# Second gate-and-up group of the second layer: each block by seven half-width block products instead of eight

## The chip, the cores and the metric

The kernel runs on one core of one Trainium2 chip. The metric is the time of one execution in microseconds; lower is better.

## The reference, cut to what matters

Two decoder layers over 512 tokens with 1024 features. Each has a mixer (attention) and then this feed-forward part, with 2816 hidden features:

```python
def swiglu(h, w_gate, w_up, w_down):
    return (jax.nn.silu(h @ w_gate) * (h @ w_up)) @ w_down

for l in range(DEPTH):
    ...
    h = x * (1.0 + sc2) + sh2
    y = swiglu(h, w_gate[l], w_up[l], w_down[l])
    x = layer_norm(ALPHA * x + (1.0 + gt2) * y, ln2_g[l], ln2_b[l])
```

## The kernel before, in words

**Data and splitting.** The input of the feed-forward part, transposed, lies in SBUF as `hT_hi` and `hT_lo` (128 partitions, 8 feature chunks `KD`, 512 tokens). Every operand of a matmul is split into a rounded high half and the remainder as low half, and a product is three matmuls: high by high, high by low, low by high (`split_product`, lines 663 to 665; `first_product`, line 1124, and `fresh_piece`, lines 727 to 732, do the same in another order). A weight piece is 128 by 1024 numbers, 512 KB. It comes by a DMA of the sync engine (SP, line 463) into one of the four slots of `w_raw`; ScalarE writes the high half `w_hi` (`convert`, line 1314; `feed`, line 1475), Vector the low half `w_lo` as raw minus high (`convert`, line 1590; `low_half` in `feed`, line 2012), and SP loads the piece four further on as soon as a piece's low half is there (`lo_ready`). TensorE marks a piece as used (`piece_used`), and only then is its slot of `w_hi` and `w_lo` written again.

**Order of the second layer's feed-forward part.** The hidden features are 22 blocks of 128, in a first group of 12 and a second of 10. Each group: `gate_up` (per block a gate piece and an up piece, each 8 chunks by 3 matmuls of 512 tokens), then two down phases, `down(l, g, 0)` and `down(l, g, 1)`, over 6 (second group 5) pieces each; a down piece is 24 matmuls of 512 columns. In a loop over pairs of blocks, `gate_up` leaves gate and up in four PSUM banks. ScalarE takes the Silu of the gate out of PSUM (line 1468) and converts the next pieces; Vector multiplies with the up block (line 2038), ScalarE rounds the result (line 1478), and Vector makes its low half (line 2043). After the first group Vector also adds the first norm's rows (`affine`, lines 1921 and 1922, with `g_row` and `b_row`), and after each down phase adds the four tiles to the residual (`residual`, lines 1845 and 1848).

**Queues.** Each engine's program is an order written out by hand; semaphores tie them. In the second layer GpSimd (POOL) has, after attention, the DMAs of the next norm's rows into `g_row` and `b_row` (`ln_rows`, lines 553 and 554) and small roots (line 496). Elsewhere it does elementwise work: the rotation of queries (`rope`, lines 426, 427, 432), the norm's rows (`affine`, lines 541 and 546) and sums of weights for the modulation (line 590). `ada_w`, a ring of four slots for modulation weights, isn't used any more in the second layer's feed-forward part.

## Time and profile before

| what | value |
|---|---|
| three runs | 1267.54, 1268.41, 1266.77 us; median 1267.54 |
| profiled execution | span 1267.1 us from the first to the last instruction; its own time beside that isn't given |
| second group of the second layer, matmuls | from about 1096.0 to 1204.8 us |
| down phases ahead of it | from about 1030 to 1096.0 us |
| instructions | 18297, of them 6362 matmuls with as many weight loads |

In rows of groups, "x20 | 24.5, 1226" is 20 instructions, 24.5 us busy, mean 1226 ns of one, and behind the next bar the idle time ahead of them and what ended it. In a timeline a row is a start and a length in us, the engine, the line of the kernel, the operation, what it writes and reads, and how many instructions are merged in it. PE is TensorE's matmuls, PEld its weight loads, DVE Vector, ACT ScalarE, POOL GpSimd, SPq the sync engine's DMA queue.

### The profile page before, as it was taken

The page shows a single profiled execution, that of the slowest core. Times are in us where ns is not written, and L with a number is a line of the kernel's source. Part 1 is how long each engine was busy: PE and PEld are TensorE (multiplying, and loading weights), DVE is VectorE, ACT ScalarE, POOL GpSimd, SP SyncE. Part 2 cuts the span into 40 slices and gives each one's busy share as a digit, 9 for nine tenths or more (in the row PEclk, how much of TensorE's full clock was granted, in tenths as well). Part 3 has the DMA queues.
Part 4 walks back from the last instruction along what each step waited for, and adds up shares of the span by engine and source line. Part 5 has one row for each costly group of instructions (what it writes and reads, how often), then busy time and mean ns, then how long its engine had stood idle before and what let it go on. Part 6 is the DMA issues. An engine that isn't in the chain of part 4 may idle for free. (4 is left out here: it accounts for less than half of the span.)

```text
span 1267.1 us, 18297 instructions
## 1 busy us (share of the span) xinstructions
PE 1230.2 (97%) x6362; PEld 1028.0 (81%) x6362; DVE 805.6 (64%) x1404; ACT 514.9 (41%) x1031; POOL 282.9 (22%) x285
## 2 busy tenths in 40 slices
PE   5999999999999999999999999899999999999997
PEld 4888887889888888888888688778988888888886
DVE  6899987777878774333776699756733355433338
ACT  4556668354333212222154566862533322222220
POOL 4247237501112010000007466670000000000000
PEclk9999999999999999999999999999999999999999
DMA  9872001424888553222523120111232223222211
GB/s 357 310 254 95 18 18 51 152 110 158 276 283 277 186 190 129 97 99 99 178 88 107 61 67 1 51 67 67 90 109 99 99 100 133 100 100 96 89 64 66
DMA packets 44849, 158.28 MB, mean 125 GB/s; under 512 B 5872, under 2 KB 5872, under 8 KB 44784
## 3 DMA queue, kind: packets, MB, share of 16 engines
q1 hardware_dynamic: 30528, 109.07, 24.6%
q0 software_dynamic: 12960, 47.19, 11.0%
q10 hardware_dynamic: 1296, 1.17, 0.3%
q8 instruction: 39, 0.64, 0.2%
q14 instruction: 26, 0.21, 0.0%
HBM read 155.31 MB, written 2.10 MB: 124 GB/s over the span
## 5 line engine op out<-in xcount | busy, mean ns | idle before, releaser
L663 PE MATMUL bank<-hT_hi,w_hi 128*128 128x512 f32 x640 | 249.4, 390 | 0.0
L665 PE MATMUL bank<-hT_hi,w_lo 128*128 128x512 f32 x640 | 249.0, 389 | 0.0
L664 PE MATMUL bank<-hT_lo,w_hi 128*128 128x512 f32 x640 | 249.0, 389 | 0.0
L2012 DVE TENSOR_TENSOR w_lo<-w_raw,w_hi 128x1024 fp32r<-128x1024 f32 x88 | 107.8, 1225 | 144.8 <-ACT w_hi L1475 144.8
L1314 ACT ACTIVATE w_hi<-w_raw 128x1024 fp32r<-128x1024 f32 x96 | 100.8, 1061 | 199.1 <-PE bank L665 184.7
L1475 ACT ACTIVATE w_hi<-w_raw 128x1024 fp32r<-128x1024 f32 x88 | 93.0, 1057 | 161.1 <-PE bank L665 155.8
L663 PE MATMUL bank<-w_hi,hT_hi 128*128 128x512 f32 (+2 forms) x392 | 148.0, 377 | 3.0 <-ACT pq L1352 2.0
L1590 DVE TENSOR_TENSOR w_lo<-w_raw,w_hi 128x1024 fp32r<-128x1024 f32 x88 | 114.1, 1311 | 56.0 <-ACT w_hi L1314 54.6
L665 PE MATMUL bank<-w_hi,hT_lo 128*128 128x512 f32 (+2 forms) x392 | 142.5, 364 | 0.0
L664 PE MATMUL bank<-w_lo,hT_hi 128*128 128x512 f32 (+2 forms) x392 | 142.4, 363 | 0.0
L664 PEld LDWEIGHTS bank<-hT_lo,w_hi 128*128 128x128 f32 x640 | 120.2, 188 | 24.9
L665 PEld LDWEIGHTS bank<-hT_hi,w_lo 128*128 128x128 f32 x640 | 120.1, 188 | 24.8
L663 PEld LDWEIGHTS bank<-hT_hi,w_hi 128*128 128x128 f32 x640 | 120.1, 188 | 24.8
L496 POOL TENSOR_TENSOR rs_out<-rs_in,minus_half 128x1 f32<-128x1 f32 x31 | 21.4, 690 | 366.6 <-DVE rs_in L1860 325.4
L663 PE MATMUL bank<-w_hi,gu_hi 128*128 128x512 f32 x264 | 102.9, 390 | 0.0
L665 PE MATMUL bank<-w_hi,gu_lo 128*128 128x512 f32 x264 | 102.7, 389 | 0.0
L664 PE MATMUL bank<-w_lo,gu_hi 128*128 128x512 f32 x264 | 102.7, 389 | 0.0
L2038 DVE TENSOR_TENSOR gu<-bank,silu_g 128x512 f32<-128x512 f32 x44 | 30.4, 692 | 95.8 <-PE bank L665 95.3
L663 PEld LDWEIGHTS bank<-w_hi,hT_hi 128*128 128x128 f32 x392 | 73.9, 188 | 21.5 <-issue 7.0
L1468 ACT ACTIVATE silu_g<-bank 128x512 f32<-128x512 f32 x44 | 26.3, 598 | 152.4 <-PE bank L665 145.9
L665 PEld LDWEIGHTS bank<-w_hi,hT_lo 128*128 128x128 f32 x392 | 73.8, 188 | 11.5
L664 PEld LDWEIGHTS bank<-w_lo,hT_hi 128*128 128x128 f32 x392 | 74.0, 189 | 9.9 <-issue 0.5
(220 smaller groups left out, 2209.9 us busy)
## 6 DMA issues: line engine op xcount, KB each, us to landing
w_raw<-in_weights SPq DMA_DIRECT2D x184, 512.0 KB, 3.5
ada_w<-in_w_ada POOLq DMA_DIRECT2D x76, 512.0 KB, 5.4
ada_w<-in_w_ada SPq DMA_DIRECT2D x4, 512.0 KB, 6.7
qT<-in_w_ada SPq DMA_DIRECT2D x4, 512.0 KB, 10.1
xs<-in_x SPq DMA_DIRECT2D x4, 512.0 KB, 16.6
g_row<-in_ln_row POOLq DMA_DIRECT2D x4, 512.0 KB, 5.2
b_row<-in_ln_row POOLq DMA_DIRECT2D x4, 512.0 KB, 6.3
trunk_out<-xs SPq DMA_DIRECT2D x8, 256.0 KB, 2.0
```

The source lines that it names most:

```text
L496: nc.gpsimd.tensor_tensor(rs_out[:, n:n + 1], rs_in[:, n:n + 1], minus_half[:], ALU.pow)\
L663: pe.matmul(dst, a_hi, b_hi, start=first, stop=False)
L664: pe.matmul(dst, a_hi, b_lo, start=False, stop=False)
L665: return pe.matmul(dst, a_lo, b_hi, start=False, stop=last)
L1314: nc.scalar.activation(w_hi[:, p % RING, :], w_raw[:, p % RING, :], ACT.Copy).then_inc(hi_ready, 1)
L1468: nc.scalar.activation(silu_g[:, f, :], bank[GU_BANK[g] + 2 * f][:], ACT.Silu)\
L1475: nc.scalar.activation(w_hi[:, s, :], w_raw[:, s, :], ACT.Copy).then_inc(hi_ready, 1)
L1590: nc.vector.tensor_tensor(w_lo[:, p % RING, :], w_raw[:, p % RING, :], w_hi[:, p % RING, :].bitcast(F32), ALU.subtract).then_inc(lo_ready, 1)
L2012: nc.vector.tensor_tensor(w_lo[:, s, :], w_raw[:, s, :], w_hi[:, s, :].bitcast(F32), ALU.subtract).then_inc(lo_ready, 1)
L2038: nc.vector.tensor_tensor(gu[:, f, :], bank[GU_BANK[g] + 2 * f + 1][:], silu_g[:, f, :], ALU.mult).then_inc(gu_ready, 1)
```

## The change

For the second layer's second group (10 blocks) `gate_up_seven` takes the place of `gate_up`. For each block the gate and up weights are seen as a 2 by 2 arrangement (gate or up, first or second half of the 1024 input features), the input as another (half of the features, half of the tokens). Eight block products of 4 chunks by 256 tokens become seven (the variant of Strassen's scheme with four sums on each side): p1 to p7 on G1, G2, U2 (halves of the weights as they are) and S1 to S4 (sums and differences of them), against halves of the input or its sums T1 to T4.

- GpSimd makes the input sums once (`input_sums`, ten operations of 1024 elements a partition, in `g_row`, `b_row` and other free space, before `ln_rows`), and four weight sums of 512 elements for each block (`weight_sums`). `ln_rows` comes behind them all.
- ScalarE and Vector split the input sums into halves (`split_input`, four each, set among the conversions of the down pieces), and for each block seven units of 512 elements (`unit`) in place of two pieces of 1024.
- TensorE does 7 products of 4 chunks by 3 matmuls of 256 columns for each block, written out without a loop; p1, p6, p7 and p4 accumulate in one bank. ScalarE copies the sum out of it after p1, p6 and p7 (`take_p1`, `take_p16`, `take_p167`), Vector adds those copies to the other products (`sum_gate1`, `sum_gate2`, `sum_up2`); Silu and multiply work on halves of 256 tokens.
- TensorE releases slots by waiting for a product of its own (`slots_used`), three times at the end.

The first layer and the first group run as before.

```diff
+SEVEN = (1,)
+SEVEN_F = FG[1]
+UNIT_ROWS = HALF
+COLS = SEQ // 2
+A_BANK, C_BANK, E_BANK = (0, 1), 2, 3
+def unit_order():
+    first = [("G1", 0), ("S2", 0), ("S3", 0), ("G2", 0), ("S1", 0), ("U2", 0)]
+    for f in range(SEVEN_F):
+        ahead = f + 1 < SEVEN_F
+        first += [("G1", f + 1)] if ahead else []
+        first += [("U2", f)] if f > 0 else []
+        first += [("S2", f + 1)] if ahead else []
+        first += [("S4", f)]
+        first += [("S3", f + 1), ("G2", f + 1), ("S1", f + 1)] if ahead else []
+    return first
+OWN_UNITS = [u for u in unit_order() if u[0] not in ("G2", "U2")]
+UNIT_SLOT = {"S2": (0, 0), "S4": (0, 1), "G1": (1, 0), "U2": (1, 1), "S3": (2, 0), "G2": (2, 1), "S1": (3, 0)}
+SUMS = ("S1", "S3", "S2", "S4")

...
+        def seven(l, g):
+            return g == 1 and l in SEVEN
...
+        def unit_raw(l, kind, f):
+            if kind in ("S1", "S3", "S4"):
+                return sum_row(kind, f)
+            s = slot(l, up_piece(f) if kind == "U2" else gate_piece(f))
+            half = int(kind in ("G2", "U2"))
+            return w_raw[:, s, half * UNIT_ROWS:(half + 1) * UNIT_ROWS]
...
+                t_op(t1_a, hi(b12), hi(b11), ALU.subtract)
+                t_op(t1_b, lo(b12), lo(b11), ALU.subtract)
+                t_op(t1_b, t1_a, t1_b, ALU.add)
+                t_op(t2_b, hi(b22), t1_b, ALU.subtract)
+                nc.gpsimd.tensor_tensor(t2_b, t2_b, lo(b22), ALU.add).then_inc(t_raw, 2)
+                pool.wait_ge(t_raw, 4 * lap7(l) + 2)
+                pool.wait_ge(gt_taken, 2 * l + 2)
+                t_op(t4_b, hi(b21), t2_b, ALU.subtract)
+                nc.gpsimd.tensor_tensor(t4_b, t4_b, lo(b21), ALU.add).then_inc(t_raw, 1)
+                t_op(own(hT_lo_raw, b12), lo(b22), lo(b12), ALU.subtract)
+                t_op(own(hT_hi_raw, b12), hi(b22), hi(b12), ALU.subtract)
+                nc.gpsimd.tensor_tensor(own(hT_lo_raw, b12), own(hT_hi_raw, b12), own(hT_lo_raw, b12), ALU.add)\
+                    .then_inc(t_raw, 1)
...
+            def weight_sums(l):
+                def free(kind, f):
+                    if f >= 2:
+                        pool.wait_ge(unit_lo, at_own(l, kind, f - 2))
+                for f in range(SEVEN_F):
+                    gate, up = w_raw[:, slot(l, gate_piece(f)), :], w_raw[:, slot(l, up_piece(f)), :]
+                    raw_ready(pool, l, up_piece(f))
+                    free("S1", f)
+                    nc.gpsimd.tensor_tensor(sum_row("S1", f), up[:, 0:HALF], up[:, HALF:PW], ALU.add)\
+                        .then_inc(weights_summed, 1)
+                    raw_ready(pool, l, gate_piece(f))
+                    free("S3", f)
+                    nc.gpsimd.tensor_tensor(sum_row("S3", f), gate[:, 0:HALF], up[:, 0:HALF], ALU.subtract)\
+                        .then_inc(weights_summed, 1)
+                    pool.wait_ge(unit_lo, at_own(l, "G1", f))
+                    pool.wait_ge(weights_summed, at_sum(l, "S3", f))
+                    nc.gpsimd.tensor_tensor(gate[:, 0:HALF], sum_row("S1", f), gate[:, 0:HALF], ALU.subtract)\
+                        .then_inc(weights_summed, 1)
+                    free("S4", f)
+                    pool.wait_ge(weights_summed, at_sum(l, "S2", f))
+                    nc.gpsimd.tensor_tensor(sum_row("S4", f), gate[:, HALF:PW], gate[:, 0:HALF], ALU.subtract)\
+                        .then_inc(weights_summed, 1)
+                pool.wait_ge(p5_done, at_f(l, SEVEN_F - 1))

...
+                    if l == 0:
+                        pool.wait_ge(unit_lo, at_own(l, "S4", SEVEN_F - 1))
+                        pool.wait_ge(p4_done, at_f(l, SEVEN_F - 1))
...
+                def product(dst, kind, f, first, last):
+                    if kind in rows:
+                        m_hi, m_lo = rows[kind]
...
+                    elif kind == "U2":
+                        pe.wait_ge(hi_ready, converted(l, up_piece(f)))
+                    else:
+                        pe.wait_ge(unit_hi, at_own(l, kind, f))
+                    for k in range(KD // 2):
+                        w = hi[:, k * P:(k + 1) * P]
+                        pe.matmul(dst, w, m_hi[:, k, :], start=first and k == 0, stop=False,
+                                  skip_group_check=not first)
+                        pe.matmul(dst, w, m_lo[:, k, :], start=False, stop=False, skip_group_check=not first)
+                    if kind == "G2":
+                        pe.wait_ge(lo_ready, converted(l, gate_piece(f)))
+                    elif kind == "U2":
+                        pe.wait_ge(lo_ready, converted(l, up_piece(f)))
+                    else:
+                        pe.wait_ge(unit_lo, at_own(l, kind, f))
+                    for k in range(KD // 2):
+                        m = pe.matmul(dst, lo[:, k * P:(k + 1) * P], m_hi[:, k, :], start=False,
+                                      stop=last and k == KD // 2 - 1, skip_group_check=not first)
+                    return m
...
+                def p7(f):
+                    if f == 0:
+                        pe.wait_ge(t_lo_ready, 4 * lap7(l) + 4)
+                    pe.wait_ge(p16_taken, at_f(l, f))
+                    product(a_sum(f), "S3", f, False, True).then_inc(p7_done, 1)
...
+                def p3(f):
+                    pe.wait_ge(up2_summed, at_f(l, f))
+                    product(e_sum, "S4", f, False, True).then_inc(p3_done, 1)
+                def slots_used(done, f, pieces):
+                    pe.wait_ge(done, at_f(l, f))
+                    nc.tensor.sem_inc(piece_used, pieces)
+                pe.wait_ge(z_done, at_z(l, DN00, T - 1))
+                for part in (p1, p2, p6, p5, p7):
+                    part(0)
+                for f in range(1, SEVEN_F):
+                    p1(f)
+                    p4(f - 1)
+                    p6(f)
+                    p3(f - 1)
+                    if f == SEVEN_F - 1:
+                        slots_used(p3_done, f - 1, 2 * SEVEN_F - 3)
+                    p7(f)
+                    p2(f)
+                    p5(f)
+                f = SEVEN_F - 1
+                p4(f)
+                slots_used(p4_done, f, 2)
+                p3(f)
+                slots_used(p3_done, f, 1)

...
+                def unit(kind, f):
+                    s, half = unit_place(kind, f)
+                    if kind in ("S1", "S3", "S2", "S4"):
+                        act.wait_ge(weights_summed, at_sum(l, kind, f))
+                    else:
+                        raw_ready(act, l, up_piece(f) if kind == "U2" else gate_piece(f))
+                    if f == 0:
+                        act.wait_ge(piece_used, used(l, GU_P[1] - RING + s))
+                    elif s == UNIT_SLOT[kind][0]:
+                        done = {"G1": p1_done, "G2": p2_done, "S4": p3_done, "U2": p4_done, "S1": p5_done,
+                                "S2": p6_done, "S3": p7_done}[kind]
+                        act.wait_ge(done, at_f(l, f - 1))
+                    nc.scalar.activation(unit_in(w_hi, kind, f), unit_raw(l, kind, f), ACT.Copy)\
+                        .then_inc(hi_ready if kind in ("G2", "U2") else unit_hi, 1)
...
+                unit("G2", 1)
+                for f in range(1, SEVEN_F):
+                    ahead = f + 1 < SEVEN_F
+                    unit("S1", f)
+                    take_p1(f)
+                    if ahead:
+                        unit("G1", f + 1)
+                    unit("U2", f)
+                    take_p16(f)
+                    if ahead:
+                        unit("S2", f + 1)
+                    unit("S4", f)
+                    silu_second(f - 1)
+                    take_p167(f)
+                    if ahead:
+                        unit("S3", f + 1)
+                    else:
+                        conv[0] += 2 * SEVEN_F
+                        convert(l, DN_P[1] + 1)
+                    high_half(f - 1)
+                    if ahead:
+                        unit("G2", f + 1)
+                    silu_first(f)
+                convert(l, DN_P[1] + 2)
+                silu_second(SEVEN_F - 1)
+                high_half(SEVEN_F - 1)

             act.dma_start(cc[:, 0, :], c_col).then_inc(c_in, 16)
...
-                feed(l, 1)
+                if l in SEVEN:
+                    for n, upto in enumerate((DN_P[0] + 8, DN_P[0] + 9, DN_P[0] + 10, GU_P[1])):
+                        convert(l, upto)
+                        split_input(l, (0, 1, 3, 2)[n])
+                    feed_seven(l)
+                else:
...
+                def sum_up2(f):
+                    dve.wait_ge(p5_done, at_f(l, f))
+                    dve.wait_ge(p167_taken, at_f(l, f))
+                    nc.vector.tensor_tensor(gu_out[:, COLS:SEQ], bank[E_BANK][:, 0:COLS],
+                                            p167_copy, ALU.add).then_inc(up2_summed, 1)
...
+                def multiply_second(f):
+                    dve.wait_ge(gate_read, gu_before(l, 1) + f + 1 + 2)
+                    dve.wait_ge(up2_summed, at_f(l, f))
+                    nc.vector.tensor_tensor(gu_out[:, COLS:SEQ], gu_out[:, COLS:SEQ], silu_out[:, COLS:SEQ],
+                                            ALU.mult).then_inc(gu_ready, 1)
+                def low_half(f):
+                    dve.wait_ge(gu_hi_ready, gu_before(l, 1) + f + 1)
+                    nc.vector.tensor_tensor(gu_lo[:, f, :], gu_out, gu_hi[:, f, :].bitcast(F32), ALU.subtract)\
+                        .then_inc(gu_lo_ready, 1)
+                    dve.wait_ge(gu_lo_ready, gu_before(l, 1) + f + 1)
...
+                    ahead = f + 1 < SEVEN_F
+                    sum_up2(f - 1)
+                    unit(l, "S1", f)
+                    if ahead:
+                        unit(l, "G1", f + 1)
+                    multiply_first(f - 1)
+                    unit(l, "U2", f)
+                    if ahead:
+                        unit(l, "S2", f + 1)
+                    sum_gate2(f - 1)
+                    unit(l, "S4", f)
+                    multiply_second(f - 1)
+                    if ahead:
+                        unit(l, "S3", f + 1)
+                    sum_gate1(f)
+                    if ahead:
+                        unit(l, "G2", f + 1)
+                    else:
+                        conv[0] += 2 * SEVEN_F
+                        convert(l, DN_P[1] + 1)
+                    low_half(f - 1)
+                f = SEVEN_F - 1
+                sum_up2(f)
+                multiply_first(f)
+                sum_gate2(f)
+                convert(l, DN_P[1] + 2)
+                multiply_second(f)
+                low_half(f)

             nc.vector.sem_inc(gu_ready, 2)
...
                 for half in range(2):
                     q = DN00 + half
-                    convert(l, PHASES[q][0] + PHASES[q][1] + (3, 2)[half])
+                    ahead = (3, 0 if l in SEVEN else 2)[half]
+                    convert(l, PHASES[q][0] + PHASES[q][1] + ahead)
+                    if l in SEVEN:
+                        for n in ((0, 1), (3, 2))[half]:
+                            split_input(l, n)
+                        if half == 1:
+                            for kind in ("G1", "S2", "S3", "G2"):
+                                unit(l, kind, 0)
                     for t in range(T):
                         residual(l, q, t, True)
                     if (l, half) == (0, 0):
                         ada_group(10)
-                convert(l, GU_P[1] + 4)
-                feed(l, 1)
+                if l in SEVEN:
+                    feed_seven(l)
+                else:
```

## Rows read from the trace of the kernel before

**Rows 1.** The page, its first line and busy time of each engine.

```profile
span 1267.1 us, 18297 instructions
...
PE 1230.2 (97%) x6362; PEld 1028.0 (81%) x6362; DVE 805.6 (64%) x1404; ACT 514.9 (41%) x1031; POOL 282.9 (22%) x285
```

**Rows 2.** Busy time by window: one loop turn of the second layer's second group.

```profile
core 0: us, PE busy (x) PEld busy (x) DVE busy (x) ACT busy (x) POOL busy (x), PEclk, DMA share, GB/s
1101.00:1122.76 21.76, 21.76 (x97) 18.02 (x96) 7.49 (x8) 6.25 (x8) 0.00 (x0) 1.00 0.40 135
```

**Rows 3.** The waits from 1096 to 1240, first and last row of seven.

```profile
DVE w_lo L2012 <- ACT w_hi L1475: 42.9, 20, 4.1
...
DVE w_lo L1590 <- ACT w_hi L1314: 3.7, 1, 3.7
```

**Rows 4.** Timeline of TensorE, 256-column matmuls of the second layer, then 512.

```profile
906.95 1.12 PE L1124 MATMUL bank<-hT_hi,w_lo 128*128 128x256 f32 x8
908.31 1.22 PE L1124 MATMUL bank<-hT_hi,w_hi 128*128 128x256 f32 x8 [0.24 <-ACT hT_hi L1337]
...
911.28 1.12 PE L1124 MATMUL bank<-hT_hi,w_hi 128*128 128x256 f32 x8
...
919.92 0.40 PE L663 MATMUL bank<-hT_hi,w_hi 128*128 128x512 f32 x1
```

**Rows 5.** Vector's group in the stretch; ScalarE's group over the span; ScalarE's timeline.

```profile
L2012 DVE TENSOR_TENSOR w_lo<-w_raw,w_hi 128x1024 fp32r<-128x1024 f32 x20 | 24.5, 1226 | 42.9 <-ACT w_hi L1475 42.9
...
L1412 ACT ACTIVATE pT<-bank 128x256 f32<-128x256 f32 x64 | 23.9, 374 | 7.0 <-PE bank L1004 7.0
...
1106.88 1.06 ACT L1475 ACTIVATE w_hi<-w_raw 128x1024 fp32r<-128x1024 f32 x1 [3.89 <-PE bank L665]
1107.85 0.61 ACT L1478 ACTIVATE gu_hi<-gu 128x512 f32 x1
```

**Rows 6.** Timelines of Vector and of GpSimd near the start.

```profile
58.49 0.69 DVE L426 TENSOR_TENSOR scratch<-bank,sin_t 128x512 f32<-128x512 f32 x1
59.09 0.68 DVE L427 TENSOR_TENSOR scratch<-bank,cos_t 128x512 f32<-128x512 f32 x1
59.81 2.51 DVE L432 TENSOR_TENSOR pq<-scratch 128x512 f32<-128x512 f32 x1
...
80.07 0.42 DVE L426 TENSOR_TENSOR gt_row<-pk,sin_t 128x256 f32<-128x256 f32 x1
80.41 0.42 DVE L427 TENSOR_TENSOR gt_row<-pk,cos_t 128x256 f32<-128x256 f32 x1
...
59.37 2.40 POOL L590 TENSOR_TENSOR g_row<-g_row,b_row 128x1024 f32<-128x1024 f32 x1 [1.26 <-ACT b_row L1372]
```

**Rows 7.** GpSimd's groups over the span.

```profile
L541 POOL TENSOR_TENSOR xs<-xs,g_row 128x512 f32<-128x512 f32 x8 | 10.1, 1282 | 0.0
...
L576 POOL TENSOR_TENSOR ada_w<-ada_w,qT 128x1024 f32<-128x1024 f32 x2 | 4.7, 2366 | 0.5 <-ACT qT L1497 0.5
```

**Rows 8.** Timeline of Vector and GpSimd side by side, 676 to 688.

```profile
677.53 8.88 DVE L1590 TENSOR_TENSOR w_lo<-w_raw,w_hi 128x1024 fp32r<-128x1024 f32 x4 [4.13 <-ACT w_hi L1314]
...
681.01 2.09 POOL L426 TENSOR_TENSOR scratch<-pq,sin_t 128x512 f32<-128x512 f32 x1
```

**Rows 9.** DMA issues from 1100 to 1200: size, median us to landing.

```profile
w_raw<-in_weights SPq DMA_DIRECT2D x19, 512.0 KB, 3.4
```

**Rows 10.** Timelines of Vector, ScalarE and GpSimd around the down phases.

```profile
1091.92 0.69 DVE L1845 TENSOR_TENSOR ztmp<-bank,gt_row 128x512 f32<-128x512 f32 x1 [4.42 <-PE bank L732]
...
1093.37 0.69 DVE L1845 TENSOR_TENSOR ztmp<-bank,gt_row 128x512 f32<-128x512 f32 x1
...
1068.86 1.06 ACT L1314 ACTIVATE w_hi<-w_raw 128x1024 fp32r<-128x1024 f32 x1 [4.38 <-PE bank L665]
...
1049.38 0.58 POOL L553 DMA_DIRECT2D g_row<-in_ln_row  x1 [149.51 <-DVE xs L1922]
...
1245.61 1.00 POOL L496 TENSOR_TENSOR rs_out<-rs_in,minus_half 128x1 f32<-128x1 f32 x1 [195.13 <-DVE rs_in L1860]
```

More of the change, by code:

```diff
@@ L554, in ln_rows, with t_op, input_sums, hi @@
                 pool.dma_start(b_row[:], ln_row[stage - 1, 1:2, :].to_broadcast([P, D_MODEL])).then_inc(row_in, 16)
+            t_steps = [0]
+            def t_op(out, a, b, op):
+                t_steps[0] += 1
+                nc.gpsimd.tensor_tensor(out, a, b, op).then_inc(t_step, 1)
+                pool.wait_ge(t_step, t_steps[0])
+            def input_sums(l):
+                def hi(block):
+                    return hT_hi[(slice(None),) + block].bitcast(F32)
+                def lo(block):
+                    return hT_lo[(slice(None),) + block].bitcast(F32)
+                pool.wait_ge(piece_used, used(l, DN_P[0] - 1))
+                pool.wait_ge(affine_done, at_tile(2 * l, T - 1))
+                def own(x, block):
+                    return x[(slice(None),) + block]
+                t_op(t1_a, hi(b12), hi(b11), ALU.subtract)
[11 more added lines that the diff above has]
+                    .then_inc(t_raw, 1)
@@ L637, in _ @@
                     base = 5 * KD + RING
-                    with pool.Fori(0, FG[0] // 2) as i:
+                    turns = FG[0] // 2 - int(0 in SEVEN)
+                    with pool.Fori(0, turns) as i:
                         for j in range(KD):
@@ L1292, in _ @@
                 for g in range(2):
-                    gate_up(l, g)
+                    if seven(l, g):
+                        gate_up_seven(l)
+                    else:
+                        gate_up(l, g)
                     down(l, g, 0)
@@ new lines, in unit @@
+            def unit(l, kind, f):
+                if kind == "G2":
+                    dve.wait_ge(hi_ready, converted(l, gate_piece(f)))
+                    dve.wait_ge(weights_summed, at_sum(l, "S4", f))
+                elif kind == "U2":
+                    dve.wait_ge(hi_ready, converted(l, up_piece(f)))
+                else:
+                    dve.wait_ge(unit_hi, at_own(l, kind, f))
+                nc.vector.tensor_tensor(unit_in(w_lo, kind, f), unit_raw(l, kind, f),
+                                        unit_in(w_hi, kind, f).bitcast(F32), ALU.subtract)\
+                    .then_inc(lo_ready if kind in ("G2", "U2") else unit_lo, 1)
```

198 lines of the change are left out of this document (195 added, 3 removed).

## The prediction

> **What bounds the kernel now.** The page comes first: TensorE is busy for 97% of the span, Vector for 64%, GpSimd for 22% [rows 1]. Then the stretch of the second layer's second gate-and-up group. Its 20 weight pieces of 24 matmuls run from about 1096.0 to 1204.8: the window of one turn of its loop (two feature blocks, 96 matmuls) is 21.76 us with TensorE busy throughout, at granted clock 1.00, the 2.4 GHz level, and GpSimd idle [rows 2]. So a feature block costs 10.88 us, a matmul 0.2267 us, the group 10 x 10.88 = 108.8 us. The waits of that stretch have no TensorE row: the other engines wait for it [rows 3]. The group is bound by matmuls, so fewer matmul columns gain, if every engine that feeds them keeps up in a shorter turn with more to do.
>
> **Matmuls.** Removed: 480 of 512 columns. Added: 7 products x 4 blocks x 3 = 84 of 256 columns per feature block, 840 in all. The column work falls by 7/8, but each matmul has a part that doesn't shrink. The trace has 256-column matmuls of the same kind, in code without a loop: from 911.28 to 919.92 nine groups of eight, 8.64 / 72 = 0.120 us each, against 0.2267 us for 512 [rows 4]. Half would be 0.1133. So a product is 12 x 0.120 = 1.44 us, a turn of seven 10.08 us, the group 100.8: **minus 8.0 us**, if nothing else counts. That the code is unrolled costs nothing in the same rows (weight loads, waits and matmuls run there without a gap). The mean duration of one (283 ns) must not be used: it overlaps the next. The Trainium skill (TensorE: Matmul & The Clock Gate, section "Wait — 56ns, not 53.3ns?") has N / 2.4 GHz + about 2.5 ns; by that the gain would be an estimated 480 x 215.8 - 840 x 109.2 ns = 11.9 us. The rows have 13 ns on top, not 2.5, and the rows count.
>
> **Three drains.** TensorE now waits three times for a product of its own before it releases slots. No row shows that. A gain is excluded; the nearest row is a wait of TensorE that ended late: 908.31 where the rhythm gave 907.91 [rows 4], 0.4 us. Bounds 0.2 (the tail 0.28 - 0.12 alone) and 0.6. I take 0.4 each, **plus 1.2 us**.
>
> **ScalarE.** Per feature block: seven conversions of 512 (0.5 us apart, half of 1024's 0.97), three copies out of PSUM and two Silu of 256 (0.37 each, an estimated 0.27 apart), one 512: 3.5 + 1.4 + 0.5 = 5.4 us of 10. It has room [rows 5]; costed at nothing, its latencies are in the turn below.
>
> **Vector.** Before: two low halves of 1024, a multiply, a low half of the product: 3.75 us of 10.88 [rows 2]. Now there are seven low halves of 512, three sums, two multiplies of 256, one low half of 512 with a wait for itself. Starts of 512-element operations lie 0.61 us apart (58.49, 59.09), of 256 ones 0.34 (80.07, 80.41) [rows 6]; with its self-wait 0.72. 7 x 0.61 + 5 x 0.34 + 0.72 = **6.7 us**. Alone that would hide.
>
> **GpSimd beside Vector.** The new sums are four GpSimd operations of 512 per feature block, 1.28 us each alone [rows 7], 5.1 of 10 us. The trace shows what two engines do to each other here: from 677.5, four Vector low halves of 1024 (1.22 us alone [rows 5]) and four GpSimd operations of 512 run side by side; Vector's take 2.22 us each, GpSimd's at least 2.09 [rows 8]. Pairs come every 2.22 us, so each GpSimd operation adds 2.22 - 1.14 = **1.08 us** to Vector's line. They take turns. In rows 6 a Vector operation with two SBUF inputs (59.81, 2.51 us instead of 0.69) waits out a GpSimd operation of 2.40; one with an input in PSUM (59.09) does not. The Trainium skill says so (SBUF — State Buffer, section "SBUF: two separate sides": the shared port pair is an exclusive lock for a Vector operation with two SBUF inputs against GpSimd); the trace agrees on who stops. What it says of the length is weighed at the rivals.
>
> **One saturated turn**, in Vector's order, from the end of G1's low half (0). The multiply of the first half, from PSUM, ends at 0.34; the S2 sum stops U2's low half until 1.3, to 1.9; the S4 sum stops S2's until 2.93, to 3.5; gate sum 3.9; S4 4.5; ScalarE's second Silu (4.0 to 4.4), multiply 4.8; ScalarE's S3 conversion (to 5.1), S3 5.8. The next up piece is fetched when U2's low half ends: 1.9 + 3.4 landing [rows 9] and two hand-overs of 0.1 give 5.6, so the S1 sum holds until 6.8, with the other gate sum hidden beside it; G2 7.4; the S3 sum holds until 8.5; product's low half 9.2; up sum 9.5; S1 10.1; G1 **10.75**. Without any stop it would be 6.7, so TensorE's 10.08 would rule. TensorE waits here, before p5 for the second gate sum and before p3 for the second up sum. Bounds of the turn: 10.08, where the stops fall into Vector's idle time, and 6.7 + 4 x 1.08 + 0.4 = 11.4, where none does; I take the schedule, since its order is fixed by the code.
>
> **Sum of the group.** 0 is the end of the down products before it. Vector's residual of tile 3 ends at 2.4 (tiles 0 to 2 earlier, they were 1.45 us each after 1091.9 [rows 10]); S1 3.0, U2 3.6, G1 of turn 1 4.2, gate sum 4.6; S4's sum holds until 6.8, S2 7.4, S1's sum 8.5, S4 9.1, S3's sum 10.2, S3 10.8, G2 11.4, up sum 11.75 (TensorE wanted it at 7.2 + 4.3 = 11.5), S1 12.4, G1 of turn 2 at 13.0. Seven such turns: 88.3. In the two last turns two and then all sums fall away; the last up sum but one is there 7.9 us later, 96.2. Then TensorE has six products, 8.6, and 1.2 of drains, one hand-over 0.2: **106.2 against 108.8, minus 2.6 us**.
>
> **Edits costed at nothing.** Ten input sums on GpSimd (1024 elements, 2.37 to 2.40 us each [rows 6, 7]) start where the row's fetch started, at 1049.4 [rows 10], and end near 1074. ScalarE then stands before its conversion of the third last down piece, which it made at 1068.9 and makes at 1075.8; TensorE, three pieces of 5.44 us behind, needs it at 1085.1. Behind that wait on Vector are the residuals of the first down half, wanted only by the group. Cover 8 us; if the ten took over 32 us, each further one would be lost. The fetch of both norm rows moves behind the group's last GpSimd sum, near 1200, and is wanted at about 1246. GpSimd's next work is at 1245.6 [rows 10]. Slots of SP's weight fetches free later within a turn but two blocks ahead. Down products after the group find their first piece converted, and have 5.44 us for each next.
>
> **Sum against the run.** Only the span, 1267.1 us, is known of the profiled execution; the median shown is 1267.54, 0.44 above. 1267.54 - 2.6 = 1264.9, given as 1265.0. A measurement here can tell 0.2%, 2.5 us, from no change.
>
> **Rivals.**
> - *TensorE stays the bound* (chance 0.25). The stops fall beside Vector's PSUM operations and waits, the turn is 10.08: 100.8 + 1.2 = 102.0, minus 6.8, 1260.7. For it: the sums can run ahead as pieces arrive. Against: Vector and GpSimd together hold 6.7 + 4.3 of a turn of 10.1.
> - *Every sum stops Vector in full* (0.20): slower. Place: Vector's line from U2 to the product's low half. If a sum holds Vector for all of its 1.28 us and not for 1.08, the turn is 4 x 0.2 longer, 11.55, and the group 7 x 0.8 = 5.6: plus 3.0, 1270.5. It decides from a turn of 11.1 on. For it: the operation at 59.81 in rows 6 ends at 62.32 and so began its own 0.69 at 61.63, only 0.14 before the GpSimd one's end. Against it: the 2.22 us rhythm of rows 8, which has the same sizes as here. The same page of the Trainium skill holds the pair "for the full instruction", which is this rival.
> - *The input sums come late* (0.05): ScalarE's wait starves the down products. With the ten at 1.5 times their duration, 36 us, it costs 4 us: 1269.
> - That the change doesn't do what it says: seven products of half width stand in the code; no chance of its own.
> The forecast has 0.50, and its own range, turn 10.4 to 11.1, is 1262.5 to 1267.5.
>
> **Numbers.** Range 1260.0 to 1270.0: the first two cases whole, the third to its middle. Faster by over 0.2%: the first rival and half of the forecast, 0.49. Within: the rest of it and some of the third, 0.31. Slower: 0.20.
>
> **What would show it.** Eight 256-column matmuls in 0.96 us; TensorE idle 0.5 to 0.8 us a turn, released by Vector's sums from PSUM (right), or none (first rival). Vector's low halves of 512 in two kinds, 0.69 and about 1.8 us. GpSimd sums above 1.28. Down products starting 106 us after the group's start. Wrong would be: matmuls at another rhythm than 0.120, idle released by ScalarE, or idle TensorE before 1096.

## The result, and the profile after

The changed kernel takes 1274.39 us (median of 4 runs, 1273.68 to 1274.59) against 1267.97 us for the kernel before in the same comparison: ratio 1.0053, 95% interval 1.0039 to 1.0068. It is 6.4 us slower, outside the range of the prediction and on the other side. Four single executions of three kernels, the one before among them, took 1380.8 to 2055.47 us and are left out of all medians here.

The page of the kernel after, its first line and the busy time of each engine (to compare with [rows 1]):

```profile
span 1272.3 us, 19331 instructions
...
PE 1227.4 (96%) x6722; PEld 1039.8 (82%) x6722; DVE 881.2 (69%) x1498; ACT 549.3 (43%) x1125; POOL 371.1 (29%) x335
```

TensorE has 360 matmuls more and yet is busy for 3 us less. Vector is busy for 76 us more. By the prediction's own figures, 6.7 us in place of 3.75 for each of ten blocks and four splits of 1.14, it would be 34. (Until the down phases the trace after runs 2.0 us ahead of the one before. The profiled execution of the kernel before was probably a slower one than its median: other executions of it took 1.6 to 2.0 us more than their spans, so its span of 1267.1 stands for about 1268.9. So stretches are compared from here on, not instants.)

**Two stretches have grown.** The down phases ahead of the group: from the same down piece to the group's first matmul it was 1079.48 to 1095.80, 16.32 us, and is now 1077.52 to 1098.68, 21.16 us: plus 4.8. The group itself: 108.8 us before, now 1098.68 to 1209.66, 111.0 us: plus 2.2. What follows the group is as long as before (62.5 and 62.6 us). The rows of the kernel before at these ends, and the one of the kernel after at the down piece:

```profile
1079.48 0.39 PE L727 MATMUL bank<-w_hi,gu_hi 128*128 128x512 f32 x1
...
1095.80 0.39 PE L663 MATMUL bank<-hT_hi,w_hi 128*128 128x512 f32 x1
...
1204.60 0.39 PE L727 MATMUL bank<-w_hi,gu_hi 128*128 128x512 f32 x1
```

```profile
1077.52 0.39 PE L918 MATMUL bank<-w_hi,gu_hi 128*128 128x512 f32 x1
```

First the group. TensorE's timeline at its start, at the rows before which it was idle in its first turns, in two middle ones (the rows up to 1193.67 are like these) and for the three drains:

```profile
1098.68 0.28 PE L1324 MATMUL bank<-hT_hi,w_hi 128*128 128x256 f32 x1
...
1100.11 0.28 PE L1324 MATMUL bank<-hT_hi,w_hi 128*128 128x256 f32 x1
...
1105.02 0.36 PE L1324 MATMUL bank<-hT_hi,w_hi 128*128 128x256 f32 x1 [0.43 <-issue]
1111.53 0.39 PE L1324 MATMUL bank<-hT_hi,w_hi 128*128 128x256 f32 x1 [0.53 <-DVE gu L2497]
...
1138.67 0.38 PE L1324 MATMUL bank<-t_hi,w_hi 128*128 128x256 f32 x1 [0.58 <-DVE silu_g L2491]
1149.67 0.39 PE L1324 MATMUL bank<-t_hi,w_hi 128*128 128x256 f32 x1 [0.58 <-DVE silu_g L2491]
...
1201.42 0.36 PE L1324 MATMUL bank<-hT_hi,w_hi 128*128 128x256 f32 x1 [0.30 <-PE bank L1334]
1207.70 0.36 PE L1324 MATMUL bank<-hT_hi,w_hi 128*128 128x256 f32 x1 [0.30 <-PE bank L1334]
1209.66 0.47 PE L918 MATMUL bank<-w_hi,gu_hi 128*128 128x512 f32 x1 [0.30 <-PE bank L1334]
```

A product of twelve matmuls takes 1.44 us (1098.68 to 1100.11). But the turn is 11.00 us, not 10.08, and before p5 TensorE waits for Vector's sum of the second gate half of the block before (L2491). Now one turn on Vector and GpSimd, by timeline:

```profile
1140.50 0.42 DVE L2485 TENSOR_TENSOR silu_g<-bank,silu_g 128x256 f32<-128x256 f32 x1
1140.93 1.36 DVE L2476 TENSOR_TENSOR w_lo<-w_raw,w_hi 128x512 fp32r<-128x512 f32 x1
1142.21 1.78 DVE L2514 TENSOR_TENSOR gu_lo<-gu,gu_hi 128x512 fp32r<-128x512 f32 x1
1144.03 0.42 DVE L2497 TENSOR_TENSOR gu<-bank,silu_g 128x256 f32<-128x256 f32 x1
1144.37 0.68 DVE L2476 TENSOR_TENSOR w_lo<-ada_w,w_hi 128x512 fp32r<-128x512 f32 x1
...
1145.91 1.67 DVE L2476 TENSOR_TENSOR w_lo<-w_raw,w_hi 128x512 fp32r<-128x512 f32 x1
1147.73 1.55 DVE L2476 TENSOR_TENSOR w_lo<-w_raw,w_hi 128x512 fp32r<-128x512 f32 x1 [0.15 <-ACT w_hi L1802]
1149.20 0.41 DVE L2491 TENSOR_TENSOR silu_g<-bank,gu 128x256 f32<-128x256 f32 x1
...
1140.31 1.43 POOL L719 TENSOR_TENSOR ada_w<-w_raw 128x512 f32<-128x512 f32 x1 [2.58 <-DMA w_raw<-in_weights]
1141.70 1.75 POOL L723 TENSOR_TENSOR ada_w<-w_raw 128x512 f32<-128x512 f32 x1
1145.73 1.30 POOL L727 TENSOR_TENSOR w_raw<-ada_w,w_raw 128x512 f32<-128x512 f32 x1 [2.29 <-DVE w_lo L2476]
1147.18 1.56 POOL L731 TENSOR_TENSOR ada_w<-w_raw 128x512 f32<-128x512 f32 x1
```

Each GpSimd sum (POOL) has one low half of Vector beside it that takes 1.36 to 1.78 us in place of 0.68. The operation at 1140.50, with an operand in PSUM, keeps its 0.42 beside the first sum. Each of the four low halves ends about 0.54 us after its sum (1140.93 + 1.36 = 1142.29, against 1140.31 + 1.43 = 1141.74), so nearly all of its own 0.68 lies behind the sum's end. And the sum at 1141.70, which met a low half already running, is itself stretched to 1.75: the two engines take turns.

Second, the down phases. Vector's timeline there, with one row of ScalarE, one of GpSimd and the one idle row of TensorE:

```profile
1064.96 3.42 DVE L2465 TENSOR_TENSOR t_lo<-b_row,t_hi 128x1024 fp32r<-128x1024 f32 x1
1068.30 3.41 DVE L2465 TENSOR_TENSOR t_lo<-t_raw,t_hi 128x1024 fp32r<-128x1024 f32 x1
1071.63 0.68 DVE L2242 TENSOR_TENSOR ztmp<-bank,gt_row 128x512 f32<-128x512 f32 x1
1072.34 2.18 DVE L2245 SCALAR_TENSOR_TENSOR xs<-xs,ztmp 128x512 f32<-128x512 f32 x1
...
1080.27 3.50 DVE L1987 TENSOR_TENSOR w_lo<-w_raw,w_hi 128x1024 fp32r<-128x1024 f32 x3
1083.68 1.22 DVE L2465 TENSOR_TENSOR hT_lo<-hT_lo_raw,hT_hi 128x1024 fp32r<-128x1024 f32 x1
...
1064.36 1.04 ACT L1608 ACTIVATE w_hi<-w_raw 128x1024 fp32r<-128x1024 f32 x1
...
1067.25 3.37 POOL L679 TENSOR_TENSOR hT_lo_raw<-hT_lo 128x1024 f32<-128x1024 f32 x1
...
1081.55 1.22 PE L923 MATMUL bank<-w_lo,gu_hi 128*128 128x512 f32 x2 [2.96 <-DVE w_lo L1987]
```

The low half of the third last down piece was made at 1080.27, though its high half was made from 1064.36 on. In the trace before it was begun 13.5 us ahead of its piece's first matmul (1079.48):

```profile
1066.01 1.23 DVE L1590 TENSOR_TENSOR w_lo<-w_raw,w_hi 128x1024 fp32r<-128x1024 f32 x1
```

In the trace after, two splits of the input sums, stopped from 1.22 (as at 1083.68) to 3.4 us each, and eight residual rows, two of them stopped from 0.69 to 2.2 and 2.05, stood before it in Vector's queue. TensorE was idle for 2.96 us. After that its granted clock fell, as busy time by windows shows (the second number from the left is the window's length, the third last the granted clock):

```profile
1079.00:1082.00 3.00, 0.45 (x1) 0.45 (x2) 2.93 (x4) 1.72 (x2) 0.00 (x0) 0.93 0.00 0
1082.00:1084.00 2.00, 2.00 (x6) 1.52 (x6) 2.00 (x3) 0.00 (x0) 0.00 (x0) 0.50 0.51 150
1084.00:1086.00 2.00, 2.00 (x9) 1.60 (x8) 2.00 (x2) 0.00 (x0) 0.77 (x1) 0.75 0.99 350
```

0.50 is the 1.2 GHz level; matmuls came every 0.43 us in place of 0.227. So the 4.8 us are 2.96 idle and 1.9 behind it, mostly this clock.

### The profile page after: what moved, and what is told of

The parts are those of the page before. It is cut to its first block and busy times, and to the rows that moved or that the text cites. A ratio compares the mean times of both kernels' runs of the same rounds, so it can differ in the third digit from the quotient of the medians.

```text
span 1272.3 us, 19331 instructions
## 1 busy us (share of the span) xinstructions
PE 1227.4 (96%) x6722; PEld 1039.8 (82%) x6722; DVE 881.2 (69%) x1498; ACT 549.3 (43%) x1125; POOL 371.1 (29%) x335
## 5 line engine op out<-in xcount | busy, mean ns | idle before, releaser
L854 PE MATMUL bank<-hT_hi,w_hi 128*128 128x512 f32 x480 | 187.1, 390 | 0.0
L856 PE MATMUL bank<-hT_hi,w_lo 128*128 128x512 f32 x480 | 186.8, 389 | 0.0
L855 PE MATMUL bank<-hT_lo,w_hi 128*128 128x512 f32 x480 | 186.8, 389 | 0.0
L1608 ACT ACTIVATE w_hi<-w_raw 128x1024 fp32r<-128x1024 f32 x96 | 100.5, 1060 | 163.5 <-PE bank L856 147.7
L2409 DVE TENSOR_TENSOR w_lo<-w_raw,w_hi 128x1024 fp32r<-128x1024 f32 x68 | 83.3, 1225 | 101.9 <-ACT w_hi L1769 101.9
L1987 DVE TENSOR_TENSOR w_lo<-w_raw,w_hi 128x1024 fp32r<-128x1024 f32 x88 | 115.6, 1329 | 41.5 <-ACT w_hi L1608 40.2
L1769 ACT ACTIVATE w_hi<-w_raw 128x1024 fp32r<-128x1024 f32 x68 | 71.9, 1057 | 122.2 <-PE bank L856 116.8
L856 PEld LDWEIGHTS bank<-hT_hi,w_lo 128*128 128x128 f32 x480 | 90.1, 188 | 18.7
L855 PEld LDWEIGHTS bank<-hT_lo,w_hi 128*128 128x128 f32 x480 | 90.1, 188 | 18.6
L854 PEld LDWEIGHTS bank<-hT_hi,w_hi 128*128 128x128 f32 x480 | 90.1, 188 | 18.4
L1697 ACT ACTIVATE pq<-pq,nmax 128x256 f32<-128x256 f32 (+3 forms) x128 | 66.6, 521 | 30.4 <-DVE nmax L2182 29.8
L822 POOL DMA_DIRECT2D ada_w<-in_w_ada x48 | 25.4, 529 | 157.5 <-DVE ada_acc L2418 55.5
```

Of the source, the lines that this page charges most:

```text
L822: pool.dma_start(ada_w[:, j % RING, :], w_ada[i + (base + j) // KD, (base + j) % KD])\
L854: pe.matmul(dst, a_hi, b_hi, start=first, stop=False)
L855: pe.matmul(dst, a_hi, b_lo, start=False, stop=False)
L856: return pe.matmul(dst, a_lo, b_hi, start=False, stop=last)
L1608: nc.scalar.activation(w_hi[:, p % RING, :], w_raw[:, p % RING, :], ACT.Copy).then_inc(hi_ready, 1)
L1697: nc.scalar.activation(p, p, ACT.Exp, scale=-1.0, bias=nmax[:, u % 2, h:h + 1], accum_out=rowsum[:, u % 2, h:h + 1]).then_inc(probs, 1)
```

## The experiments

Theory A: an instruction of GpSimd that reads two operands from SBUF and one of Vector that does the same take turns. That stretches Vector's turn in the group, and in the down phases it makes one low half late. The rivals: B, Vector and ScalarE are short of time whatever GpSimd does; F, the sums are simply late, in the loop of fetch, sums, conversions and release of the slot; for the down phases C, ScalarE's waits for the input sums, and D, the order of Vector's queue. All times are medians, each beside the kernel before on the same chip (1267.3 to 1268.3).

### The weight sums made small

```diff
-nc.gpsimd.tensor_tensor(sum_row("S1", f), up[:, 0:HALF], up[:, HALF:PW], ALU.add)
+nc.gpsimd.tensor_tensor(sum_row("S1", f)[:, 0:8], up[:, 0:8], up[:, HALF:HALF + 8], ALU.add)
```

and the same for S3, S2 and S4.

> GpSimd's four weight sums of each block are done on 8 of their 512 elements: 504 of the elements of S1, S3, S2 and S4 are left out, everything else (waits, conversions, products, Vector's residuals) stays. Theory A, the sums hold up Vector's instructions with two SBUF operands: Vector's low halves go back from 3.36 to about 1.22 us for two and 1.78 to 0.6 for one, the turn from 11.0 to 10.1 us (7 x 1.44, TensorE-bound), the group from 111.0 to 102 to 103 us, the time to 1266. Theory B, the turn is set by the amount of work on Vector and ScalarE and by the semaphores between them, whatever GpSimd does: the turn stays at 10.8 to 11.0 us and the time at 1273 to 1274. The stall ahead of the group (2.96 us and the matmuls of 0.43 us behind it) stays with both.

1265.73 us, ratio 0.9982 (0.9973 to 0.9991). The group runs from 1099.10 to 1201.42, 102.3 us, with no idle row of TensorE but those of the three drains. B falls. But a sum of 8 elements is both short for Vector and early for the rest, so A and F are not told apart yet.

### As late as a sum, without its reads

```diff
+for _ in range(2):
+    nc.gpsimd.memset(sum_row("S1", f), 0.0).then_inc(t_step, 1)
+    t_steps[0] += 1
+    pool.wait_ge(t_step, t_steps[0])
 nc.gpsimd.tensor_tensor(sum_row("S1", f)[:, 0:8], up[:, 0:8], up[:, HALF:HALF + 8], ALU.add)
```

and the same for S3, S2 and S4.

> Each of GpSimd's four weight sums becomes two fills of the same 512 elements with zeros and then the sum on 8 elements (the rest of S1, S3, S2 and S4 is left out). So what follows a sum gets it as late as before, 2 x 0.6 + 0.3 = 1.4 to 1.5 us (a fill took 0.53, with its hand-over 0.6; a sum of 8 elements 0.2, with its hand-over 0.28), but GpSimd reads two operands from SBUF for 0.2 us only. Theory A, the reading of two SBUF operands stops Vector's instructions that read two as well, and the turn is Vector's own 7.1 us plus its waits plus these stops: the turn is 10.1 us, Vector busy 7.1 to 7.5 of it, the time 1265.5 to 1267. Rival F, what counts is that each sum comes 1.3 us later in a loop of fetch, sums, conversions and release of the slot: the turn stays at 10.9 to 11.4 us and the time at 1273 to 1277, as with the full sums.

1266.00 us, ratio 0.9984 (0.9975 to 0.9993), as with the small sums. The sums' places in GpSimd's timeline, and one turn by windows:

```profile
1144.98 1.11 POOL L720 MEMSET ada_w<- 128x512 f32 x2 [2.01 <-DMA w_raw<-in_weights]
1146.17 0.20 POOL L723 TENSOR_TENSOR ada_w<-w_raw 128x8 f32<-128x8 f32 x1
```

```profile
1130.00:1140.08 10.08, 10.08 (x86) 10.08 (x85) 7.12 (x14) 6.38 (x14) 4.96 (x13) 1.00 0.35 104
```

The same turn of the kernel after:

```profile
1138.70:1149.70 11.00, 10.42 (x85) 10.18 (x85) 10.46 (x14) 6.21 (x14) 6.00 (x4) 1.00 0.34 102
```

GpSimd is busy for 4.96 us of the turn (6.00 with full sums), and S1 is ready 1.4 us after its start, as late as before. Yet Vector's same 14 instructions take 7.12 us and not 10.46, and TensorE is busy throughout. What costs is the reading, not the lateness: A is shown for the group, F falls. (Whether a GpSimd operation that reads one operand would stop Vector too, no run shows.)

By busy time the stops are 10.46 - 7.12 = 3.3 us a turn, 0.84 for each sum. That is a little low: with gaps between them, as here, Vector's operations are counted with their tails, which the next one covers where they stand close. By the starts of the rows after, the four low halves take 1.28, 1.82, 1.82 (0.23 of it waiting) and 1.47 us until the next operation begins, in place of 0.61, 0.72, 0.61 and 0.61: 3.6 us, 0.9 for each sum. The Trainium skill (SBUF — State Buffer, section "Terms") has the pair of ports "held for the full instruction". The rows agree on who stops whom, and on the length as well, since each low half ends only 0.54 us after its sum. That a sum of 1.28 us costs only 0.9 on average is because two of the four start beside an operation from PSUM (1140.31 beside 1140.50), and one runs in part while Vector waits for ScalarE (before 1147.73).

### One sum more, and its control

The extra sum is S1 done twice; the control fills S1's place with zeros ahead of it.

> GpSimd does S1 of each block twice (a fifth sum per turn, same operands, same result, waited for before the next). Theory A, each GpSimd sum with two SBUF operands takes its length away from Vector's line while Vector is saturated: a turn goes from 11.0 us to 11.0 plus 1.1 to 1.3, and with eight saturated turns the group from 111.0 to about 120, the time from 1274.4 to 1283 (1282 to 1285). Theory B, GpSimd has time to spare (5.5 us of its sums in a turn of 11.0) and Vector is limited by its own chain of waits: no change, 1274 to 1275.

> The control for the extra sum: ahead of S1 GpSimd fills S1's place with zeros (an instruction that reads no operand from SBUF and writes the same 512 elements), and the real sum follows. Theory A, what stops Vector is a GpSimd instruction that reads two operands from SBUF: little or nothing, turn 11.0 to 11.2 us, 1274.4 to 1276. If any GpSimd instruction stops Vector for its length, or if only S1's later arrival counts, it is as in the run with the extra sum, 1280 or more.

1280.69 us (ratio 1.0104, 1.0088 to 1.0119) and 1277.01 us (1.0073, 1.0058 to 1.0089). One turn of each by windows, first the extra sum:

```profile
1130.65:1142.29 11.64, 10.42 (x85) 10.19 (x85) 11.10 (x14) 6.23 (x14) 7.66 (x5) 1.00 0.26 92
```

```profile
1129.99:1141.40 11.41, 10.59 (x84) 10.18 (x84) 10.87 (x14) 6.22 (x14) 6.37 (x5) 1.00 0.26 90
```

The turn is always Vector's busy time and 0.54 us in which it is idle, 0.49 of them in waits for ScalarE: 10.46, 11.10 and 10.87 give 11.00, 11.64 and 11.41. So Vector sets the turn. Both sizes were missed. The fifth sum adds 0.64 us a turn and not 1.1 to 1.3: the last of the three sums in a row (1135.38 to 1137.13) lies beside an operation from PSUM first (1136.01), and the low half behind that takes 1.33 us in place of 0.68. And the fill, which stops nobody, still adds 0.4, more than the 0.2 that theory A allowed and less than the 0.64 of the sum. It starts S1's sum 0.6 us later, and a low half that lay half beside that sum (1.36 us) now lies wholly beside it (1.69 to 1.83). Where a sum falls in Vector's order counts, not only how many there are.

### Fewer input sums

```diff
-t_op(t1_a, hi(b12), hi(b11), ALU.subtract)
-t_op(t1_b, lo(b12), lo(b11), ALU.subtract)
-t_op(t1_b, t1_a, t1_b, ALU.add)
+t_op(t1_b, hi(b12), hi(b11), ALU.subtract)
...
```

> Four of the ten input sums are done in the down phases, six are left out (T1, T2 and T4 get one half each, T3 one difference), so what the group multiplies is other data of the same shape. Theory A, the input sums hold up Vector's splits and residual sums and so make one low half of a down piece late: with four sums of 2.4 us only one split or so is held, TensorE's wait of 2.96 us shrinks below 1 us, its granted clock does not fall to 0.50, and the down phases before the group get 3 to 5 us shorter: 1269.5 to 1271. Theory C, ScalarE's waits for the sums (9.86 and 11.42 us) are the cause: the same saving, but Vector's splits stay at 3.4 us. Theory D, only the order of Vector's queue matters: no change, 1274. The group stays at 111.0 us with all.

1270.20 us, ratio 1.0022 (1.0011 to 1.0032). TensorE has no idle row in the down phases and its clock stays at 1.00; the group starts at 1093.94, 4.7 us earlier, and is 111.0 us long as before. The two splits take 1.21 us each. So the input sums cause the 4.8 us, but this run stops Vector less and frees ScalarE earlier at once.

### The order of Vector's queue

```diff
 for n in ((0, 1), (3, 2))[half]:
     split_input(l, n)
+if half == 0:
+    convert(l, PHASES[q][0] + PHASES[q][1] + 4)
```

> One conversion of Vector in the down phases (the low half of the next down piece) is put ahead of the two residual additions, right behind the two splits; nothing else changes. Theory A with D: the low half that was there at 1080.27 us lands 4.2 us earlier (the two residual additions of 2.18 and 2.05 us now follow it), TensorE's 2.96 us and the slow clock behind it go, the group starts about 4.5 us earlier, 1269.5 us; the group itself stays 111.0. Theory C, ScalarE's late sums: ScalarE's conversions were ready only 2.5 us before the low half, so the stall ends there and the gain is at most 2.5 us, 1272; the reduction that follows the residuals could also come 1.2 us later and take part of it back.

1272.99 us, ratio 1.0047 (1.0034 to 1.0061). The stall is gone with all ten sums in place and ScalarE's waits as they were: the group starts at 1094.20, 4.5 us earlier. So C falls and D holds. That the stops (A) are needed as well is worked out, since no run takes them alone away here: without them the low half would have come by about 1073 (1064.96, two splits of 1.14, eight rows of 0.72), in time; with them it is in time only ahead of the rows. But of the 4.5 us only 1.4 was left in the medians, and 1.6 in the trace; the intervals of this ratio and of the changed kernel's overlap. TensorE's idle rows at the group's start:

```profile
1101.17 0.74 PE L1334 MATMUL bank<-t_hi,w_lo 128*128 128x256 f32 x4 [1.54 <-DVE w_lo L2476]
1103.48 0.35 PE L1324 MATMUL bank<-hT_hi,w_hi 128*128 128x256 f32 x1 [1.57 <-issue]
```

Vector was still behind by what the stops had cost (with four input sums, at the same start of the group, the wait before the fifth product was 0.43 us), and GpSimd's weight sums fell on it there, two low halves of 1.77 us right ahead of the group; the granted clock was 0.50 again from 1105 to 1107. The group took 113.9 us.

### The weight sums on Vector

```diff
-nc.gpsimd.tensor_tensor(sum_row("S1", f), up[:, 0:HALF], up[:, HALF:PW], ALU.add)
+nc.vector.tensor_tensor(sum_row("S1", f), up[:, 0:HALF], up[:, HALF:PW], ALU.add)
...
+sum_pair(l, f + 1)
 unit(l, "G1", f + 1)
+sum_s2(l, f + 1)
 multiply_first(f - 1)
+sum_s4(l, f + 1)
```

`sum_pair` makes S1 and S3, the others S2 and S4, each with the waits that it needs.

> The four weight sums of each block are done by Vector instead of GpSimd, right ahead of the residual that needs them; GpSimd does the input sums alone. Theory A: a sum of 512 by 512 elements takes Vector about 0.6 us when GpSimd is still, so a turn of Vector holds 6.7 + 4 x 0.6 = 9.1 us, below TensorE's 10.1; the turn becomes 10.1 to 10.3 us, the group 102 to 104, and the time 1266 to 1268. Theory B, Vector is short of time or latency whoever does the sums: with 2.4 us more work on it the turn rises to 11.5 us or more and the time to 1277 or above.

1267.25 us, ratio 0.9996 (0.9988 to 1.0005), 7.1 us below the changed kernel. The group is 104.1 us (1098.40 to 1202.48) and has, beside those of the drains, one idle row, of 1.56 us, before its fifth product.

### Both, and the fifth product

The next three runs join the new order with the sums on Vector, and then move Vector's first sum of gate halves:

```diff
+sum_gate1(0)
 sum_pair(l, 1)
 unit(l, "G1", 1)
 sum_s2(l, 1)
-sum_gate1(0)
 sum_s4(l, 1)
```

> The weight sums on Vector and the conversion put ahead of the residual additions, together. Theory A: the two savings are of different stretches, so they add: with the sums on Vector the time was 1267.3, with the order changed the group started 4.5 us earlier but its first turns gave 2.9 of that back while GpSimd's weight sums and Vector's backlog met; with no weight sums on GpSimd the backlog is worked off by the group's start, so all 4.5 stay: 1262.5 to 1263.5. Theory E, Vector's backlog at the group's start is what is short and the order only moves the wait: 1265.5 to 1267.

> As the run before, and Vector's first sum of gate halves (the one that frees the bank which the fifth product writes) goes ahead of G1(1)'s low half and of S2's sum. In the run with the sums on Vector the fifth product started 0.8 us after the end of that sum, 1.7 us late (1105.87 instead of 1104.16). Expected: that sum ends 1.3 us earlier, the fifth product starts at most 0.4 us late, 1.3 us less than the run before: 1261 to 1262. If the bank is not what it waits for, no change to the run before.

> As the run with the first sum of gate halves ahead of G1(1)'s low half (1263.3 us, the fifth product 1.6 us late), but that sum goes ahead of S1(1) and S3(1) too, 1.2 us earlier on Vector. If the fifth product starts 0.8 us after its end, it is now 0.4 us late and not 1.6: 1262.0 (1261.5 to 1262.6). If the bank is not what it waits for any more: 1263.3.

The first gives 1266.17 us (ratio 0.9987, 0.9978 to 0.9996), 3 us more than theory A wanted: the down phases keep their gain, but the fifth product now waits 2.93 us. Theory E was nearer. With the sum between, 1263.29 us (0.9964, 0.9951 to 0.9977); with it in front, 1262.36 us (0.9961, 0.9947 to 0.9974), the lowest median of this study, 5.3 us below the kernel before. (The last two can't be told apart by their times: 1262.13 to 1264.09 and 1262.12 to 1264.00.) The row before which TensorE waits, in the first, second and third:

```profile
1102.62 0.35 PE L1302 MATMUL bank<-hT_hi,w_hi 128*128 128x256 f32 x1 [2.93 <-issue]
```

```profile
1102.76 0.36 PE L1302 MATMUL bank<-hT_hi,w_hi 128*128 128x256 f32 x1 [1.62 <-issue]
```

```profile
1102.12 0.36 PE L1302 MATMUL bank<-hT_hi,w_hi 128*128 128x256 f32 x1 [0.40 <-issue]
```

The profile names no releaser, but the row begins 0.8 us after the end of Vector's first gate sum in every run. Of the 1.2 us by which the last step shortened this wait the group kept only 0.3 (104.1 and 103.9 us): three waits of about 0.2 to 0.4 us came up within the next 11 us. The profile of the fastest shows a turn of 10.08 us, TensorE busy throughout:

```profile
1130.00:1140.08 10.08, 10.08 (x86) 10.08 (x85) 9.66 (x19) 6.73 (x14) 0.00 (x0) 1.00 0.35 106
```

Vector does 19 instructions in place of 14 here and is busy for 9.66 us in place of 10.46: four sums done by Vector (0.6 us each) cost it less than four done beside it by GpSimd.

### The first layer too

> The same kernel as the run before, with the second group of the first layer done in seven products too (weight sums on Vector, the conversion ahead of the residual additions, the first gate sum early). Theory A: the group of the first layer gains what the second's gains, 108.8 to 103 us, so 5 to 6 us less than the run before: 1256 to 1257.5. Rival: in the first layer Vector also has the rows of the modulation to add in these phases and GpSimd the sums aside for it, so Vector is late into the group: 1259 to 1264.

1270.25 us, ratio 1.0019 (1.0010 to 1.0028): a loss of 7.9 us against the run before. The first layer's group runs well, but TensorE waits ahead of it:

```profile
486.43 1.22 PE L901 MATMUL bank<-w_lo,gu_hi 128*128 128x512 f32 x2 [10.90 <-DVE w_lo L1965]
```

It is again a low half of a down piece behind the residual rows in Vector's queue, now the next piece's, with eight rows of the modulation between as well. So those conversions went ahead of the rows:

```diff
 if (l, half) == (0, 0):
+    convert(l, PHASES[DN01][0] + PHASES[DN01][1])
     ada_group(10)
```

> Both layers' second groups in seven products, as the run before, with one thing changed: in the first layer Vector makes the low halves of the next two down pieces ahead of its eight modulation rows (9.2 us from 473.7 to 485.2), behind which one of them landed so late that TensorE waited 10.90 us. Their high halves were there by 471.8, before those rows began. Theory D, the queue order on Vector: the 10.90 us go, and what is left is a later G1(0) (its high half waits on ScalarE behind the same rows), 1 to 2 us: 1259.5 to 1261.5, so 1 to 3 us below the kernel with the second layer alone. Rival: the stall moves whole to the group's first product, which needs units made behind those rows: 1266 to 1270.

1270.87 us, ratio 1.0030 (1.0018 to 1.0041): the rival. The wait moved to the group's first products, five idle rows of 9.0 us together. TensorE at the group's first product, and ScalarE:

```profile
489.50 0.55 PE L1302 MATMUL bank<-hT_hi,w_hi 128*128 128x256 f32 x1 [4.74 <-ACT w_hi L1780]
```

```profile
487.79 1.06 ACT L1763 ACTIVATE t_hi<-scratch 128x1024 fp32r<-128x1024 f32 x1 [16.73 <-DVE ada_acc L2011]
```

ScalarE may not write T4 before the modulation's ring, whose memory T4 uses, is read out, and stands there for 16.73 us with the group's first units behind it. Another place for T4, or the rows earlier, wasn't tried.

## Why the prediction was wrong

**Matmuls and drains: right.** 1.44 us a product and 10.08 a turn where nothing else counts. The three drains came 0.46 us late each against 0.4 predicted. Without the stops the group takes 102.3 us (predicted 100.8 + 1.2 = 102.0).

**One saturated turn: right in kind, 0.25 too short.** The prediction named the engine, the reason and the place (idle of 0.5 to 0.8 before p5, released by Vector's sum): 0.58 us, and 11.00 us against 10.75, within the forecast's own 10.4 to 11.1. Its schedule holds 6.7 of Vector's own work, 3.75 of stops and 0.3 of waiting; by the starts of the rows it was 6.7, 3.6 and 0.7. What was short is the waiting, nearly all of it for ScalarE: it was counted before S3 (0.3, measured 0.42) and not before S2 (0.23) and G2 (0.09).

**Sum of the group: the sign was wrong through three terms.** Its 106.2 became 111.0. G1 of turn 2 had its low half at 13.9 and not 13.0 (0.9); seven turns took 77.0 and not 75.3 (1.7); and the end took 20.1 and not 17.9 (2.2): the last wait was not for the last up sum but one, with six products behind it, but before the ninth block's p5 for the eighth block's second gate sum (1193.67), with ten. Each is small; together they outweigh the 2.6 us that were to be gained. The rival with the longer turn, "every sum stops Vector in full", had the sign and nearly the size (plus 3.0, measured 2.2), but by the wrong term: a sum does hold a low half nearly to its end, yet the turn was 11.00 and not 11.55, and the rest is at the group's two ends. That its number lay near is luck.

**Edits costed at nothing: the step that failed most.** The ten input sums were judged by ScalarE's wait, with 8 us of cover, and Vector's rows behind it were called "wanted only by the group". ScalarE's part held: it made that conversion at 1077.79, 5 us before its piece was due (that is the second last down piece, which the prediction calls the third last), and the run with the changed order had no stall with ScalarE as late. What was missed is that these rows, and the splits, stand in Vector's queue ahead of the low half of the piece before that, which TensorE wants at 1078.6 (1081.55 less its 2.96 of idle time), and that the same turn-taking that was worked out for the group holds here too, with sums twice as long: two splits of 3.4 us in place of 1.2, two residual rows of 2.2 and 2.05 in place of 0.69. The rival "the input sums come late" named the sums and the place, but as ScalarE's wait and at 0.05. And the price of the idle time was not only 2.96 us: the clock fell behind it, 1.9 more.

The sum: 4.8 of the stall and 2.2 of the group, 7.0 by these stretches; 6.4 between the medians. (That the traced execution before was the one of 1267.54, 0.44 above its span, was assumed and is unlikely, but no term hangs on it.) "Idle TensorE before 1096" stood among the signs that would make the prediction wrong, and it is what is seen.

## What to carry to other kernels

Work moved to an idle GpSimd is not free for Vector when both read two operands from SBUF: count the GpSimd time as Vector's wherever Vector is busy, in every stretch that it runs in, and look what stands behind it in Vector's queue. If Vector would need half the time for the same sum, give it to Vector. When an engine's queue holds work of two due times, put the piece that TensorE wants next first, and then follow the backlog to the place where it is paid.

## What the runs showed of the hardware

- A granted clock that fell after a short wait. Idle rows of 1.56 and 1.62 us before the fifth product left it at 1.00. After 2.93 us at the same place, it was 0.50 in the window from 1104 to 1106, and the group took 106.9 us (1093.78 to 1200.71) against 104.1 with 1.62 us: 1.3 us of the difference are idle time, 1.5 the clock. In the run with only the order changed, two idle rows of 1.54 and 1.57 us within 2.3 us brought it to 0.50 as well.
- A fill of 512 elements by GpSimd (0.53 us) does not stop Vector (its busy time for the 14 instructions is 7.12 us with 2 fills in each sum's place, and 7.12 with neither fills nor full sums); a sum of 512 (1.28 us) stops a low half to as much as 1.78 us and is itself stretched to 1.75, and one of 1024 (2.4 us) stops a low half of 1024 to 3.4.
- Vector's operations with an operand in PSUM kept 0.41 to 0.42 us for 256 elements beside any GpSimd sum.
